# Recurrent mixer: two low halves on GpSimd, transfers reordered, last places filled by halves

## The chip, the cores and the metric

The kernel runs on one core of a Trainium2 chip. The metric is the device time of one execution in microseconds. The engines are TensorE (PE, with its weight loads as PEld), VectorE (DVE), ScalarE (ACT), GpSimd (POOL) and SyncE (SP), which issues all transfers.

## The reference

The reference is a stack of layers over x of 1 x 256 x 1024 in float32. First block: a mixer "ab", a routed feed-forward (moe0), a recurrent mixer (lru), a second routed feed-forward (moe1). Second block: twice a dense feed-forward, a pooling and attention mixer, and another dense feed-forward. The part around the change is:

```
# recurrent mixer: h = rms_norm(x)
gate, xr = split(h @ w_in); gate = gelu(gate)
xr = causal_conv(xr, conv_w) + conv_b              # 4 taps
r = sigmoid(xr @ w_a per head + b_a); i = sigmoid(xr @ w_x per head + b_x)
log_a = 8 r log_sigmoid(lam); a = exp(log_a)
b = sqrt(-expm1(2 log_a)) * (i * xr)
h_t = a_t h_{t-1} + b_t                            # over 256 positions
x = x + (gate * h) @ w_out
# routed stage: h = rms_norm(x); one group of 4, top 2 of its 8 experts
x = x + sum over the chosen experts of gate_e * (silu(h @ Wg_e) * (h @ Wu_e)) @ Wd_e
```

Each routed stage has 32 experts with three matrices of 2 MB each.

## The kernel before

Everything lives in SBUF with the channels on the 128 partitions. Dense weights come in chunks of 1 MB (`dense_chunks`, keys such as `("lru", 10)`), through a ring of six places: chunk number n lies in place n % 6. A chunk that is used in split precision is rounded by ScalarE to a high half (`hi`, L1238) and gets its low half by subtraction on VectorE (`lo`, L1670). `hi` counts `rounded` up, `lo` counts `remainder` up, per half f of the chunk, and TensorE then makes three products for each tile (`tile_products`, L570). The halves of the chunks of ab and lru lie in two pairs of buffers in turn. The chunks lru 8 and 9 are used as loaded, without halves (`whole_by_rows`, L775).

The lru stage: chunks lru 0 to 3 make the recurrent branch's input, `c_w_a` and `c_w_x` its gates, lru 4 to 7 the gelu branch, lru 8 to 11 the output projection. lru 4 to 7 lie in places 2 to 5, lru 8 to 11 in places 0, 1, 2 and 3. TensorE goes through lru 4 to 7 with the gates' products between them, then lru 8 and 9 together (L785: products for k 0 to 3 need gy 0 and gy 1, k 4 and 5 need gy 2, k 6 and 7 need gy 3), then lru 10 and lru 11. `gated(g)` on VectorE (L1876) makes gy g from the gelu branch (ScalarE, L1398) and the scan (L1913). All engines run in program order. VectorE's order at the end of the stage is scan 0, scan 1, gated 0, scaled_gate 3, gated 1, scan 2, gated 2, lo of lru 10 and 11, scan 3, gated 3, and then the low halves of gy. ScalarE's is four roots, four gelus, hi of lru 10 and 11, and the high halves of gy.

The routed stages read their 96 matrices each in a fixed order through about 13 places of 2 MB: expert rings, `work`, `spare_place`, and pairs of places of the dense ring (`EXTRA`, L464). `PLACES` (L470) lists which place each matrix takes. SyncE issues all of it in one order (`sp_program`, L2434): each issue waits until the last reader of its place is done. For the second routed stage it issues lru 4 to 7 with matrices 0 to 3 between them; then lru 8, 9, 10, 11 (`dense_load`, L2447; lru 8 and 9 wait for the gates' products, L2456); then matrix 4 when the low halves of lru 6 and 7 are made, 5 when those of lru 10 and 11 are made, 6 (in `work`) when all of gy and lru 9 are used, 7 when lru 8 and 9 are used, 8 and 9 after the products of lru 10 and 11 (`OUT_CHUNKS`, L465). The issues at L2490 are quarters of matrices that go out as TensorE frees parts of matrix 0. TensorE's products of the experts are L860 (gate, up) and L869 (down).

GpSimd does two sums at each routed stage (`first_sums`, L2419) and small work in the attention mixers.

Of the kernel before, what the change touches and what calls it, by code (L numbers as in the profile page):

```python
# [5 lines left out]
F32 = mybir.dt.float32  # L6
# [170 lines left out]
def build(nc, a, out, known):  # L177
# [14 lines left out]
    vec = signal("vec")  # L192
# [177 lines left out]
    for key in halved:  # L370
        held_before[key] = held_by.get(halves_of[key])
        held_by[halves_of[key]] = key
    splits = set(halved)

# [75 lines left out]
    def pair(ap, q):  # L452
        return ap[:, 2 * q:2 * q + 2, :]
# [79 lines left out]
    def pe_program(_):  # L533
# [36 lines left out]
        def tile_products(key, b, ready, x=h_halves, ks=range(KD), between=None):  # L570
            w = weights(key)
            for f in range(2):
                if f and between:
                    between()
                PE.wait_ge(remainder, key, f)
                for n, k in enumerate(ks):
                    PE.wait_ge(*ready(k))
                    ins = triple(bank[b][:, f * T:(f + 1) * T], [v[:, f, k, :] for v in w],
                                 [v[:, k, :] for v in x], n == 0, n == KD - 1)
                ins.then_inc(products.up(key, f), 1)  # L580
# [648 lines left out]
    def act_program(_):  # L1229
# [112 lines left out]
        def lru():  # L1342
            whole("lru")
            hi(("lru", 1))
            for q in range(4):
                gained("lru", q)
            table(ACTF.Sqrt)
            squares("lru")
            hi(("lru", 2))
            rms_later("lru", 3)  # L1350
            hi(("lru", 3))

            def first_tap(j):
                ACT.wait_ge(vec, "xr_in", j)
                for c in (2 * j, 2 * j + 1):
                    ins = S.activation(lru_xr[:, c, :], lru_pad[:, c, 0:T], ACTF.Identity, bias=small_of("c_conv_b", c, 1),
                                       scale=small_of("c_conv_w", c, 1))
                ins.then_inc(acted.up("tap", j), 1)

            def gates(g):  # L1360
                for m in range(2):
                    ACT.wait_ge(products, "gate", g, m)
                    ACT.wait_ge(vec, "half_b")
                    for f in range(2):
                        h = 2 * g + f
                        ins = S.activation((lru_ra, lru_bx)[m][:, h, :], bank[GATE_BANK[g % 2][m]][:, f * T:(f + 1) * T],
                                           ACTF.Tanh, bias=lru_cst[:, 4 + m, h:h + 1], scale=0.5)
                    ins.then_inc(acted.up("tanh", g, m), 1)
                ACT.wait_ge(acted, "tanh", g, 0)
                for h in (2 * g, 2 * g + 1):  # L1370
                    less = lru_cst[:, 1, h:h + 1]
                    ins = S.activation(hT[:, h, :], lru_ra[:, h, :], ACTF.Tanh, bias=less, scale=less)
                ins.then_inc(acted.up("less", g), 1)
                ACT.wait_ge(acted, "less", g)
                for h in (2 * g, 2 * g + 1):
                    c = lru_cst[:, 0, h:h + 1]
                    ins = S.activation(lru_ra[:, h, :], lru_ra[:, h, :], ACTF.Exp, bias=c, scale=c)
                ins.then_inc(acted.up("ra", g), 1)

            first_tap(0)  # L1380
            hi(("lru", 4))
            first_tap(1)
            table(ACTF.Tanh)
            hi(("lru", 5))
            gates(0)
            first_tap(2)
            first_tap(3)
            gates(1)
            hi(("lru", 6))
            gates(2)  # L1390
            hi(("lru", 7))
            gates(3)
            for g in range(4):
                ACT.wait_ge(vec, "factor", g)
                S.activation(pair(hT, g), pair(hT, g), ACTF.Sqrt).then_inc(acted.up("root", g), 1)
            for j in range(4):
                ACT.wait_ge(vec, "scaled_gate", j)
                S.activation(pair(lru_gate, j), pair(lru_gate, j), ACTF.Gelu_apprx_tanh).then_inc(acted.up("gelu", j), 1)  # L1398
            hi(("lru", 10))
            hi(("lru", 11))  # L1400
            for g in range(4):
                ACT.wait_ge(vec, "gy", g)
                ACT.wait_ge(products, ("lru", 7), 1)
                S.copy(pair(h_halves[0], g), pair(lru_gate, g)).then_inc(rounded.up("gy", g), 1)
            project("lru", 8, [])
# [263 lines left out]
    def dve_program(_):  # L1669
        def lo(key, halves=(0, 1)):  # L1670
            for f in halves:
                DVE.wait_ge(rounded, key, f)
                V.tensor_tensor(half_of(key, f, 1), tile_of(slot(key), key, f), half_of(key, f, 0).bitcast(F32),  # L1673
                                ALU.subtract).then_inc(remainder.up(key, f), 1)
# [158 lines left out]
        def lru():  # L1833
# [86 lines left out]
            gated(1)  # L1920
            scan(2)
            gated(2)
            lo(("lru", 10))
            lo(("lru", 11))
            scan(3)
            gated(3)
            for g in range(4):
# [470 lines left out]
    def pool_program(_):  # L2398
        def pools(s):

            POOL.wait_ge(vec, "ss", s)
            if s == "m1":
                POOL.wait_ge(vec, "merged", "m0", 3)
            for buf in (uT, s2, s4):
                ins = G.memset(buf[:, :, 0:EDGE], 0.0)
            pool_seq(ins, "edges", s)
            POOL.wait_ge(vec, "u", s, 4)
            src, dst = uT, s2
            for n, w in enumerate(WINDOWS):
                sh = w // 2  # L2410
                pool_seq(G.tensor_tensor(dst[:, n:, EDGE:L], src[:, n:, EDGE:L], src[:, n:, EDGE - sh:L - sh], ALU.add))
                G.tensor_scalar(poolT[:, n, EDGE:], dst[:, n, 2 * EDGE:L], 1.0 / w, None, ALU.mult)
                pool_seq(G.tensor_tensor(poolT[:, n, 0:EDGE], dst[:, n, EDGE:2 * EDGE],
                                         C("rcount")[:, n * EDGE:(n + 1) * EDGE], ALU.mult))
                pool_seq(G.tensor_tensor(poolT[:, n, :], poolT[:, n, :], uT[:, n, EDGE:L], ALU.subtract),
                         *(("pool", s) if n == 3 else ()))
                src, dst = dst, (s4 if dst is s2 else s2)

        def first_sums(s):  # L2419

            q = [work[:, EXP_F + i * 2 * T:EXP_F + (i + 1) * 2 * T] for i in range(3)]
            POOL.wait_ge(acted, "sq", s, 1)
            pool_seq(G.tensor_tensor(square_sum, q[0], q[1], ALU.add))
            POOL.wait_ge(acted, "sq", s, 2)
            pool_seq(G.tensor_tensor(square_sum, square_sum, q[2], ALU.add), "ss", s)

        for s in ROUTED:
            first_sums(s)
        for s in LATER:
            if s[0] == "m":  # L2430
                pools(s)


    def sp_program(_):  # L2434
# [128 lines left out]
        done = RING  # L2563
        for l in range(2):
            last = order.index(("ab", 13) if l == 0 else ("lru", 11)) + 1
            for i, n in enumerate(range(done, last)):
                dense_load(n)
                if i < 4:

                    if l:  # L2570
                        SP.wait_ge(products, *last_of(0, *PLACES[1][0][i]))
                    experts(l, i, i + 1)
            done = last
            n = 4
            for i, both in enumerate(EXTRA[l]):
                for d in both:
                    old = [k for k in order[:last] if place_of[k] == d][-1]
                    SP.wait_ge(products if old in AS_LOADED else remainder, old, 1)
                experts(l, n, n + 1)
                n += 1  # L2580
                if i == l:

                    if l == 0:
                        SP.wait_ge(remainder, "y", 3)
                    else:
                        SP.wait_ge(remainder, "gy", 3)
                        SP.wait_ge(products, ("lru", 9), 1)
                    experts(l, n, n + 1)
                    n += 1
            for i, key in enumerate(OUT_CHUNKS[l]):  # L2590
                SP.wait_ge(products, key, 1)
                experts(l, n, n + 1)
                n += 1
            second_half_of_first(l)
            last_quad = N_MATRIX - 2 * RING
            experts(l, n, last_quad)
            SP.wait_ge(vec, "flag", l)
            again(l, sync.value_load(most_tokens[0:1, l:l + 1], min_val=0, max_val=T))
            experts(l, last_quad, N_MATRIX)
            next_chunks(l, done, done + RING)  # L2600
            done += RING
# [71 lines left out]
```

## Time and profile before

| | us |
|---|---|
| median of 3 runs | 2076.36 |
| lowest and highest run | 2074.45, 2080.01 |
| the profiled execution | 2074.32 |
| its span | 2072.4 |
| PE, DVE, ACT, POOL busy | 1843.8, 1014.7, 703.5, 39.2 |
| mean transfer rate | 302 GB/s |

The profile is of one execution, its times counted from the start of the span. The lru stage lies from about 540 to 621 us, the second routed stage from there to about 1064 us. A busy share of TensorE near 1 does not say that TensorE is at its peak.

### The profile page before, as it was taken

The numbers are of one execution on the slowest core, as the hardware profiler recorded it, in microseconds if no ns is written. First come the engines' busy times: TensorE is split into PE (matmuls) and PEld (weight loads), VectorE is DVE, ScalarE is ACT, GpSimd is POOL, SyncE is SP. The second block draws the span as 40 slices with busy tenths as digits, with TensorE's granted clock in tenths as the row PEclk, the third lists the DMA queues.
The fourth block names the chain that finished last, engine by engine and source line by source line (L and its number), as shares of the span: only waits on it lengthen the run. The fifth ranks groups of instructions, "written<-read, shape, count | busy, mean of one in ns | idle before, by whom it ended". The sixth has DMA issues, their size and how long they took to land.

```text
span 2072.4 us, 31532 instructions
## 1 busy us (share of the span) xinstructions
PE 1843.8 (89%) x13948; PEld 1438.9 (69%) x13948; DVE 1014.7 (49%) x1434; ACT 703.5 (34%) x1049; POOL 39.2 (2%) x46
## 2 busy tenths in 40 slices
PE   9987776676998866677799999999999999999999
PEld 7944433344894433343478889998888888999888
DVE  5722110111672111011158777877777667787666
ACT  6310000000651000000055555655546445465553
POOL 0000000000000000000000003000000000300000
PEclk9999999989999999899899999999999999999999
DMA  9899999999979999999985554545555556445552
GB/s 397 338 415 429 430 430 431 430 429 425 407 323 419 430 430 429 430 431 430 426 326 194 192 207 174 182 170 185 184 204 193 190 183 216 175 160 183 186 195 88
DMA packets 64654, 626.59 MB, mean 302 GB/s; under 512 B 7168, under 2 KB 7296, under 8 KB 14464
## 3 DMA queue, kind: packets, MB, share of 16 engines
q1 hardware_dynamic: 64512, 624.50, 75.6%
q8 instruction: 113, 1.85, 0.3%
q14 instruction: 29, 0.24, 0.0%
HBM read 623.42 MB, written 1.05 MB: 301 GB/s over the span
## 4 chain that ended last, share of the span: by engine, by line
PE 72%; DMA 19%; DVE 4%; ACT 2%; SPq 2%; issue 1%; DVEq 0%; ACTq 0%
PE ps L606 14%; PE ps L609 7%; DMA dense_ring<-in_moe_w_down 7%; PE ps L869 7%; PE ps L550 6%; PE ps L552 6%; PE ps L551 6%; DMA expert_ring_a<-in_moe_w_down 5%; PE ps L860 5%; PE ps L1093 4%; PE ps L1072 4%; DMA work<-in_moe_w_down 3%; PE ps L849 3%; PE ps L885 3%; PE ps L1077 2%; PE ps L1097 2%
## 5 line engine op out<-in xcount | busy, mean ns | idle before, releaser
L1673 DVE TENSOR_TENSOR w_lo<-dense_ring,w_hi 128x1024 fp32r<-128x1024 f32 x398 | 468.9, 1222 | 54.8 <-ACT w_hi L1246 53.7
L1246 ACT CAST w_hi<-dense_ring 128x1024 fp32r<-128x1024 f32 x398 | 397.0, 1048 | 47.2 <-PE ps L552 26.1
L606 PE MATMUL ps<-h_both,w_hi 128*128 128x512 f32 x1344 | 337.3, 393 | 0.8 <-DVE work L2152 0.8
L606 PEld LDWEIGHTS ps<-h_both,w_hi 128*128 128x128 f32 x1344 | 241.8, 189 | 45.5 <-DVE work L2152 2.2
L2019 DVE TENSOR_TENSOR work<-work,ps 128x256 f32<-128x256 f32 x32 | 13.5, 421 | 484.4 <-ACT work L1437 484.4
L609 PEld LDWEIGHTS ps<-h_both,w_lo 128*128 128x128 f32 x1344 | 183.3, 190 | 13.1
L550 PE MATMUL ps<-h_both,w_hi 128*128 128x256 f32 x656 | 188.5, 287 | 0.4 <-DVE h_both L1679 0.3
L609 PE MATMUL ps<-h_both,w_lo 128*128 128x256 f32 x1344 | 187.4, 282 | 0.0
L552 PE MATMUL ps<-h_both,w_lo 128*128 128x256 f32 x656 | 185.6, 283 | 0.0
L551 PE MATMUL ps<-h_both,w_hi 128*128 128x256 f32 x656 | 185.6, 283 | 0.0
L1437 ACT ACTIVATE work<-ps 128x256 f32<-128x256 f32 x32 | 12.3, 384 | 484.6 <-PE ps L860 484.6
L860 PE MATMUL ps<-expert_ring_a,work 128*32 128x256 f32 x1216 | 114.6, 449 | 53.7 <-DMA expert_ring_a<-in_moe_w_up 29.2
L869 PE MATMUL ps<-dense_ring,work 128*32 128x512 f32 (+1 forms) x400 | 124.7, 559 | 16.3 <-DMA expert_ring_b<-in_moe_w_down 7.7
L550 PEld LDWEIGHTS ps<-h_both,w_hi 128*128 128x128 f32 x656 | 125.8, 192 | 1.9 <-DVE h_both L1679 0.8
L551 PEld LDWEIGHTS ps<-h_both,w_hi 128*128 128x128 f32 x656 | 125.8, 192 | 0.2
L552 PEld LDWEIGHTS ps<-h_both,w_lo 128*128 128x128 f32 x656 | 125.7, 192 | 0.0
L860 PEld LDWEIGHTS ps<-expert_ring_a,work 128*32 128x32 f32 x1216 | 61.2, 129 | 92.8 <-issue 74.2
L2152 DVE TENSOR_TENSOR work<-ps,work 128x512 f32<-128x512 f32 x87 | 60.1, 690 | 106.7 <-ACT work L1509 106.3
L860 PE MATMUL ps<-expert_ring_b,work 128*32 128x256 f32 x1088 | 88.1, 397 | 19.9 <-DMA expert_ring_b<-in_moe_w_gate 6.3
L869 PE MATMUL ps<-expert_ring_b,work 128*32 128x512 f32 (+1 forms) x288 | 92.1, 575 | 15.2 <-DMA expert_ring_b<-in_moe_w_down 9.3
L1509 ACT COPY work<-ps 128x512 f32<-128x512 f32 x87 | 50.9, 585 | 154.5 <-PE ps L609 154.1
L860 PE MATMUL ps<-dense_ring,work 128*32 128x256 f32 x992 | 99.3, 392 | 3.7 <-ACT work L1452 3.7
(319 smaller groups left out, 2852.1 us busy)
## 6 DMA issues: line engine op xcount, KB each, us to landing
dense_ring<-in_dense SPq DMA_DIRECT2D x207, 1024.0 KB, 4.9
expert_ring_b<-in_moe_w_up SPq DMA_DIRECT2D x20, 2048.0 KB, 39.9
expert_ring_a<-in_moe_w_gate SPq DMA_DIRECT2D x19, 2048.0 KB, 42.7
expert_ring_a<-in_moe_w_up SPq DMA_DIRECT2D x19, 2048.0 KB, 41.4
dense_ring<-in_moe_w_down SPq DMA_DIRECT2D x17, 2048.0 KB, 35.7
dense_ring<-in_moe_w_gate SPq DMA_DIRECT2D x17, 2048.0 KB, 39.9
expert_ring_b<-in_moe_w_down SPq DMA_DIRECT2D x14, 2048.0 KB, 44.8
dense_ring<-in_moe_w_up SPq DMA_DIRECT2D x14, 2048.0 KB, 40.0
```

The costliest lines, as they stand in the source:

```text
L550: mm(o, w[0], x[0], start=start, stop=False, **kw)
L551: mm(o, w[0], x[1], start=False, stop=False, **kw)
L552: return mm(o, w[1], x[0], start=False, stop=stop, **kw)
L606: mm(bank[b + f], w[0][:, f, k, :], h_pairs[:, k, :], start=k == 0, stop=False)
L609: ins = mm(bank[b + f][:, 0:T], w[1][:, f, k, :], h_halves[0][:, k, :], start=False, stop=k == KD - 1)
L849: ins = mm(bank[b][:, (k % 4) * P:(k % 4 + 1) * P], h_tok[:, tt * D + k * P:tt * D + (k + 1) * P], pick[:, tt * P:(tt + 1) * P], start=tt ...
L860: ins = mm(bank[2 + pr][c:c + CAP, m * half:(m + 1) * half], xs[:, k, (2 * pr + x) * CAP:(2 * pr + x + 1) * CAP], w[:, k, hf * half:(hf + ...
L869: return mm(bank[b][r0:r0 + CAP, cols], hidT[pr][:, c:c + CAP], w[:, parts, f, :], start=f == 0, stop=f == FE - 1)
L1072: mm(bank[4 + dt], w[0][:, f, dt * P:(dt + 1) * P], hid_pairs[:, 4 * j + f, :], start=j == f == 0, stop=False, skip_group_check=True)
L1093: mm(bank[E_BANK[s][c][f]], w[0][:, f, k, :], hid_pairs[:, r * KD + k, :], start=r == k == 0, stop=False, skip_group_check=True)
L1246: S.copy(half_of(key, f, 0), tile_of(slot(key), key, f)).then_inc(rounded.up(key, f), 1)
L1673: V.tensor_tensor(half_of(key, f, 1), tile_of(slot(key), key, f), half_of(key, f, 0).bitcast(F32), ALU.subtract).then_inc(remainder.up(key ...
```

## The change

Three things. The low halves of lru 10 and 11 are made by GpSimd instead of VectorE, and ScalarE rounds lru 10 ahead of its four gelus. SyncE issues lru 10 and 11 ahead of lru 8 and 9. And in the second routed stage matrix 5 is issued as two halves, the first when the low halves of lru 10 are made and the second when those of lru 11 are; the second half of matrix 6 goes out between them, after the last scan, and its first half where all of matrix 6 went. For the first routed stage the order is written anew but the same.

```diff
+    LESS_BY_POOL = [("lru", 10), ("lru", 11)]
 def tile_products(...)
-                PE.wait_ge(remainder, key, f)
+                PE.wait_ge(pooled if key in LESS_BY_POOL else remainder, key, f)
 ScalarE, lru()
+            hi(("lru", 10))
             for j in range(4):
                 ACT.wait_ge(vec, "scaled_gate", j)
                 S.activation(pair(lru_gate, j), pair(lru_gate, j), ACTF.Gelu_apprx_tanh)...
-            hi(("lru", 10))
             hi(("lru", 11))
 VectorE, lru()
             gated(2)
-            lo(("lru", 10))
-            lo(("lru", 11))
             scan(3)
 GpSimd
+        def less_of(key):
+            for f in range(2):
+                POOL.wait_ge(rounded, key, f)
+                G.tensor_tensor(half_of(key, f, 1), tile_of(slot(key), key, f), half_of(key, f, 0).bitcast(F32),
+                                ALU.subtract).then_inc(pooled.up(key, f), 1)
         for s in ROUTED:
+            if s == "moe1":
+                for key in LESS_BY_POOL:
+                    less_of(key)
             first_sums(s)
 SyncE
-            for i, n in enumerate(range(done, last)):
+            for i, n in enumerate(range(done, last) if l == 0 else [*range(done, last - 4), last - 2, last - 1, last - 4, last - 3]):
                 dense_load(n)
...
+            def emptied(d):
+                old = [k for k in order[:last] if place_of[k] == d][-1]
+                SP.wait_ge(products if old in AS_LOADED else pooled if old in LESS_BY_POOL else remainder, old, 1)
+            def by_halves(n, both, between=None):
+                for h, d in enumerate(both):
+                    emptied(d)
+                    piece(l, n, h, 2)
+                    if between and h == 0:
+                        between()
+            def late_work(n):
+                SP.wait_ge(vec, "scan", 7)
+                piece(l, n, 1, 2, last=0)
+            (first, second, third), w = EXTRA[l], n + 1 + l
...
+            else:
+                emptied(first[0])
+                emptied(first[1])
+                experts(l, n, n + 1)
+                by_halves(n + 1, second, lambda: late_work(w))
+                SP.wait_ge(remainder, "gy", 3)
+                SP.wait_ge(products, ("lru", 9), 1)
+                piece(l, w, 0, 2, last=0)
+            emptied(third[0])
+            emptied(third[1])
+            experts(l, n + 3, n + 4)
+            n += 4
```

## Rows read from the trace of the kernel before

**Rows 1.** The page, part 2: transfer rate in 40 equal slices of the span.
```profile
GB/s 397 338 415 429 430 430 431 430 429 425 407 323 419 430 430 429 430 431 430 426 326 194 192 207 174 182 170 185 184 204 193 190 183 216 175 160 183 186 195 88
```

**Rows 2.** Stretches: length, busy us of PE, PEld, DVE, ACT, POOL, clock, DMA share, GB/s.
```profile
574.50:579.50 5.00, 5.00 (x38) 4.79 (x37) 4.83 (x8) 4.97 (x10) 0.00 (x0) 1.00 0.08 20
...
594.50:599.50 5.00, 5.00 (x25) 4.40 (x24) 4.96 (x6) 2.12 (x4) 0.00 (x0) 1.00 0.04 16
...
605.00:607.00 2.00, 2.00 (x19) 2.00 (x18) 1.30 (x3) 0.63 (x1) 0.51 (x1) 1.00 0.73 156
607.00:633.00 26.00, 23.73 (x213) 20.88 (x213) 10.60 (x45) 7.00 (x15) 2.07 (x2) 1.00 1.00 425
633.00:636.00 3.00, 3.00 (x46) 2.15 (x50) 0.00 (x0) 1.93 (x3) 0.00 (x0) 1.00 0.83 270
...
700.00:1040.00 340.00, 244.30 (x2216) 130.47 (x2216) 40.42 (x84) 13.88 (x30) 0.00 (x0) 0.89 1.01 429
```

**Rows 3.** The chain of waits in the second routed stage: start, us, what.
```profile
897.71 36.49 DMA dense_ring<-in_moe_w_down
```

**Rows 4.** SyncE's longest wait (us, times, longest), then its issues: start, us, what.
```profile
SPq L2461 <- PE ps L753: 23.6, 1, 23.6
...
578.42 2.03 SPq L2461 DMA_DIRECT2D dense_ring<-in_dense  x4
...
605.03 0.33 SPq L2470 DMA_DIRECT2D work<-in_moe_w_gate  x1
...
610.73 7.87 SPq L2470 DMA_DIRECT2D expert_ring_b<-in_moe_w_up  x2
...
618.27 0.33 SPq L2470 DMA_DIRECT2D expert_ring_b<-in_moe_w_up  x1
...
630.89 0.33 SPq L2490 DMA_DIRECT2D expert_ring_a<-in_moe_w_down  x1
```

**Rows 5.** ScalarE, 583 to 596 us, in order of time: start, us, what.
```profile
586.61 1.28 ACT L1398 ACT_TABLE_LOAD   x1
587.90 1.67 ACT L1398 ACTIVATE work<-work 128x512 f32<-128x512 f32 x3
...
591.20 3.87 ACT L1246 CAST w_hi<-dense_ring 128x1024 fp32r<-128x1024 f32 x4
```

**Rows 6.** VectorE, 588 to 602 us, in order of time.
```profile
588.87 0.67 DVE L1876 TENSOR_TENSOR work<-work 128x512 f32<-128x512 f32 x1
...
593.85 4.63 DVE L1673 TENSOR_TENSOR w_lo<-dense_ring,w_hi 128x1024 fp32r<-128x1024 f32 x4
...
600.49 0.69 DVE L1876 TENSOR_TENSOR work<-work 128x512 f32<-128x512 f32 x1
```

**Rows 7.** TensorE, products of lru 8 and 9, then the first of lru 10.
```profile
589.73 10.55 PE L785 MATMUL ps<-work,dense_ring 128*128 128x256 f32 x48
601.23 3.72 PE L785 MATMUL ps<-work,dense_ring 128*128 128x256 f32 x16 [0.95 <-DVE work L1876]
604.60 0.47 PE L550 MATMUL ps<-h_both,w_hi 128*128 128x256 f32 x1
```

**Rows 8.** First attention mixer: GpSimd and VectorE in order of time; GpSimd's sums by line.
```profile
1275.02 1.89 POOL L2411 TENSOR_TENSOR scratch<-scratch 128x1024 f32<-128x1024 f32 x1 [23.76 <-DVE scratch L2340]
...
1275.10 3.17 DVE L2265 TENSOR_TENSOR scratch<-scratch,work 128x1280 f32<-128x1280 f32 x1
...
L2423 POOL TENSOR_TENSOR work<-work 128x512 f32<-128x512 f32 x2 | 2.6, 1291 | 600.3 <-ACT work L1252 600.3
```

**Rows 9.** Transfers issued at 598.5, 618.3 and 630.9 us: KB, us from issue to landing.
```profile
dense_ring<-in_moe_w_down SPq DMA_DIRECT2D x1, 2048.0 KB, 8.0
...
expert_ring_b<-in_moe_w_up SPq DMA_DIRECT2D x1, 2048.0 KB, 9.9
...
expert_ring_a<-in_moe_w_down SPq DMA_DIRECT2D x1, 512.0 KB, 6.4
```

More of the change, by code:

```diff
@@ L2574, in sp_program @@
             n = 4
[L2575 to L2578, printed above, removed]
-                experts(l, n, n + 1)
[L2580 to L2589, printed above, removed]
+            def emptied(d):
[11 more added lines that the diff above has]
+            (first, second, third), w = EXTRA[l], n + 1 + l
+            if l == 0:
+                emptied(first[0])
+                emptied(first[1])
+                experts(l, n, n + 1)
+                SP.wait_ge(remainder, "y", 3)
+                experts(l, w, w + 1)
+                emptied(second[0])
+                emptied(second[1])
+                experts(l, n + 2, n + 3)
+            else:
+                emptied(first[0])
+                emptied(first[1])
+                experts(l, n, n + 1)
[7 more added lines that the diff above has]
+            n += 4
             for i, key in enumerate(OUT_CHUNKS[l]):
```

## The prediction

> **What bounds the kernel now.** I read the rate of the transfers over the span first. In the first half the core loads at about 430 GB/s in most slices, in the second half at about half that [rows 1]. The change lies in the recurrent mixer (540 to 621 us), ahead of the second routed stage. That stage is bound by loading: from 700 to 1040 us the DMA engines are busy without a gap at 429 GB/s while TensorE works 244.30 of 340 us [rows 2], and the chain of waits goes through transfers of 36 us each, once per quad of experts [rows 3]. So its end is the end of one stream of transfers. A microsecond in which that stream stands still is lost, unless the stream is held up again later for a reason that the change does not touch: then only the last hold-up counts.
>
> The stretches [rows 2] show where it stands still: 5.0 us at 20 GB/s, 5.0 us at 16 GB/s and 2.0 us at 156 GB/s. Against 429 GB/s that is 4.8 + 4.8 + 1.3 = 10.9 us. From 607 to 633 us it runs at 425 GB/s, and from 633 to 636 us at 270 GB/s once more (3.0 x (1 - 270/429) = 1.1 us).
>
> SyncE's queue tells why [rows 4]. It stood 23.6 us in one wait, for the gates' products, and issued nothing until 578.42 us; then it waited for low halves of chunks (matrix 5 goes out at 598.5 us) and for output products (605.03, 610.73, 618.27 us). The issue at 630.89 us waits for TensorE's first expert products.
>
> **The change, part by part.** (1) Chunks lru 10 and 11 are issued ahead of lru 8 and 9. Their places were emptied by the low halves of lru 4 and 5, which VectorE makes before `factors(0)`, long before 578 us. Two chunks are 2.1 MB, 4.9 us at 429 GB/s: they run in the first hole. lru 8 and 9 come next and start no later than now, since their own wait sets them. Gain in the stream at this point 4.8 us.
>
> (2) ScalarE rounds lru 10 before the gelus. The roots end at 586.6 us, a table load of 1.28 us follows, and the gelus start at 587.90 us [rows 5]. Two roundings of 0.97 us each (3.87 for four) go in front: table load 588.6 to 589.9, first gelu done at about 590.5. VectorE's `gated(0)`, now started at 588.87 us [rows 6], waits for it. Without more, gy 0 is there at 591.2 instead of 589.5 us, and TensorE, which starts the output products at 589.73 us with no gap [rows 7], starts 1.5 us later. Queued behind this wait on VectorE are `scaled_gate(3)`, `gated(1)` and the scans.
>
> (3) VectorE loses four subtractions, 4.63 us [rows 6]. `gated(3)`, now at 600.49 us, moves forward by it. TensorE waits for it only 0.95 us, between its 48 and its last 16 matmuls [rows 7]: this is all that TensorE can gain from part 3. With parts 2 and 3 alone it reaches lru 10 at 604.60 + 1.5 - 0.95 = 605.1 us, 0.5 us late.
>
> (4) GpSimd makes the four halves. No row has this shape on it; the nearest two: 128x1024 in 1.89 us, and 128x512 in 1.29 us, twice that is 2.6 us [rows 8]. I take 1.9, the row of the same size, and keep 2.6 as the other end. Their own end (about 600 us) is early enough for TensorE, which needs them after 604 us. What matters is what they do to VectorE. VectorE's 128x1280 instruction started 0.08 us after GpSimd's 1.89 us one and took 3.17 us [rows 8]; at the 1.16 us per 1024 of the four subtractions [rows 6] it takes 1.5 alone. It stood still for 1.7 us: the two engines did not read together, and VectorE waited out the whole GpSimd instruction. Nearly all of VectorE's instructions here (scan, `gated`) have both inputs in SBUF, as that one had; `scaled_gate`, from PSUM, has one.
>
> [...]
>
> So, in turn: the first high half is rounded at 587.6; GpSimd gets in when the running scan ends, 588.3, and holds until 590.0; VectorE's last scan of the pair runs to 590.6; GpSimd's second holds until 592.3; `gated(0)` ends at 592.95. TensorE starts at 593.0 instead of 589.73: 3.3 us. It needs gy 2 after 7.0 us (600.0) and gy 3 after 10.55 us (603.5). VectorE and GpSimd take turns again for lru 11 (rounded at 595.2 and 596.1, since the fourth gelu goes first): gy 2 at about 600.0, gy 3 at 602.9, in time. TensorE is late by 3.3 - 0.95 = 2.3 us. With the 2.6 us price `gated(0)` ends 1.4 us later, gy 2 comes at about 603.0 against 601.4 needed and gy 3 at about the end of those products, less the turns: 5.3 us late. Without the exclusion 0.5.
>
> (5) Places filled by halves. First half of matrix 5 at about 592.4, second half of matrix 6 after the last scan (602), second half of 5 at about 602, first half of 6 with the wait for lru 9. Each issue costs SyncE 0.33 us, and it is otherwise waiting. These 3 MB fill part of the second and third hole.
>
> What is late next decides. Matrix 8 and 9 and the pieces at 630.89 us are issued when TensorE is done, so these move with it. How much was in the queue then? An issue into an empty queue takes 8.0 us to land (2 MB, 598.5 us); the one at 618.27 us took 9.9: it found 1.9 us of work ahead. The 512 KB at 630.89 us took 6.4 [rows 9]; an empty queue would be 8.0 less 1.5 MB at 429 GB/s (3.7), 4.3 to 4.9: at most 2.1, 1.5 likely. But the rate fell to 270 GB/s just there, which says the queue was running dry: 0 is the other end. I take 0.8. A fuller stream ahead of 618 us can therefore not be carried past 631 us by more than that reserve. Whatever the holes give beyond is lost again, as an empty queue that waits for TensorE.
>
> **Sum.** Stream end after = +(TensorE's delay) - (reserve) = 2.3 - 0.8 = +1.5 us. Ends: 0.5 - 1.5 = -1.0 and 5.3 - 0 = +5.3. Later stages are unchanged and follow. The profiled execution took 2074.32 us (span 2072.4, 1.9 outside): 2075.8. The median shown is 2.0 us higher, 2076.36, within the 5.6 us between its runs; I forecast for it 2077.9 us. About 0.3% (6.2 us) is what a measurement can tell from no change: this is no change.
>
> **Rivals.** A: the hole counts in full. All 10.9 us come out (2065.5), or the 4.8 of part 1 (2071.6). For it: the stage is bound by the stream. Against it: the reserve at 618.27 and 630.89 us, which only an earlier TensorE can raise, and TensorE can gain 0.95 at most. 4 in 100.
> B: slower. The exclusion is dearer: GpSimd's instructions hold 2.6 us or get in before each of VectorE's, so that gy 0, gy 2 and gy 3 are each late. The price is 5.3 us on the forecast's side of the reserve, 2081.7; it counts from a delay of TensorE above the reserve, and passes 0.3% above 7 us. For it: the 1.29 us row. 14 in 100.
> C: no exclusion for scans, or GpSimd in the gaps of VectorE: delay 0.5, -1.0 to +0.5, 2075.4 to 2076.9. Against it the 3.17 us row. 16 in 100.
> D: the change does not do what it says: lru 10 lands or is rounded no earlier in effect (its half place in ScalarE's order still waits for lru 6's products), and all stays within 0.5 us of 2076.4. Against it: those products end near 584 us. 4 in 100.
>
> **How the numbers follow.** Forecast 62 in 100; its own range 2076 to 2080. The range 2073.4 to 2082 takes in C, D and B's price, and the runs' own spread; A and the worst of B are outside. Faster by over 0.3%: A's upper half and stray runs, 0.03. Slower: B beyond 7 us and stray runs, 0.07. Same: 0.90.
>
> **What would show it.** Step 1: no hole at 574 to 579 us. Step 2: first gelu about 2 us later. Step 4: scans or `gated` of VectorE that take 2 us and more beside GpSimd; four GpSimd rows of about 2 us. TensorE's first output product near 593 us and no gap of 0.95 us before the last 16. The holes at 594 and 605 us smaller, a new one near 620 or a longer one near 634 us. From 700 us on the same picture shifted by 1 to 2 us. I am wrong if the second routed stage ends over 2 us earlier, or if TensorE is more than 5 us late at lru 10.

## The result, and the profile after

The changed kernel takes 2080.43 us (median of 13 runs, 2079.47 to 2082.57), the one before 2075.36 us over 13 runs beside it (2073.14 to 2080.01). The ratio, formed from the runs beside each other, is 1.0026, 95% interval 1.0018 to 1.0033: 5.4 us slower. That is just under the 0.3% (6.2 us) named in the prediction, and with this many runs clear of zero. The time lies in the range of 2073.4 to 2082 us, but 0.4 us above the forecast's own 2076 to 2080; the forecast 2077.9 us had 1.5 of the 5.4 us.

The span went from 2072.4 to 2077.9 us. The first view is the one of stretches, of the kernel after; its columns are those of [rows 2].

```profile
574.50:579.50 5.00, 5.00 (x38) 4.79 (x37) 4.83 (x8) 4.97 (x10) 0.00 (x0) 1.00 0.97 377
594.50:599.50 5.00, 5.00 (x13) 3.98 (x12) 4.86 (x5) 3.09 (x5) 3.82 (x2) 0.50 0.36 149
599.50:605.00 5.50, 5.50 (x27) 4.83 (x27) 5.36 (x7) 1.54 (x3) 1.27 (x1) 1.00 0.17 31
607.00:633.00 26.00, 25.65 (x189) 23.87 (x188) 9.96 (x35) 5.22 (x10) 2.58 (x2) 0.93 0.93 371
...
637.00:639.00 2.00, 2.00 (x25) 1.30 (x24) 0.91 (x5) 0.37 (x1) 0.00 (x0) 1.00 0.70 256
700.00:1040.00 340.00, 248.92 (x2236) 133.12 (x2232) 40.40 (x84) 13.85 (x30) 0.00 (x0) 0.88 1.01 429
```

The first hole is filled: 377 GB/s where it was 20. The stream stands still later instead, 31 GB/s from 599.5 to 605 us, where it ran at 372 before, and from 607 to 633 us it moves 371 GB/s against 425. From 700 us on it is busy at 429 GB/s, as before. New is TensorE's clock: 0.50 from 594.5 to 599.5 us, where it was 1.00 before. The 0.93 in the stretch from 607 to 633 us is a second, shorter fall, from 626.9 to 630.1 us.

The next fences are VectorE, GpSimd and ScalarE of the kernel after, in order of time (start, us, what); they answer to [rows 6], [rows 8] and [rows 5].

```profile
587.21 5.61 DVE L1914 TENSOR_TENSOR_SCAN work<-work 128x256 f32<-128x256 f32 x2
592.74 0.66 DVE L1877 TENSOR_TENSOR work<-work 128x512 f32<-128x512 f32 x1
593.33 0.68 DVE L1881 TENSOR_TENSOR work<-ps,rinv 128x512 f32<-128x512 f32 x1
...
595.24 3.39 DVE L1914 TENSOR_TENSOR_SCAN work<-work 128x256 f32<-128x256 f32 x2
598.73 2.59 DVE L1877 TENSOR_TENSOR work<-work 128x512 f32<-128x512 f32 x1
...
603.33 0.69 DVE L1877 TENSOR_TENSOR work<-work 128x512 f32<-128x512 f32 x1
```

```profile
587.18 2.39 POOL L2430 TENSOR_TENSOR w_lo<-dense_ring,w_hi 128x1024 fp32r<-128x1024 f32 x1 [494.30 <-ACT w_hi L1247]
589.54 2.73 POOL L2430 TENSOR_TENSOR w_lo<-dense_ring,w_hi 128x1024 fp32r<-128x1024 f32 x1
595.68 2.40 POOL L2430 TENSOR_TENSOR w_lo<-dense_ring,w_hi 128x1024 fp32r<-128x1024 f32 x1 [3.41 <-ACT w_hi L1247]
```

```profile
586.01 1.98 ACT L1247 CAST w_hi<-dense_ring 128x1024 fp32r<-128x1024 f32 x2
588.01 1.28 ACT L1400 ACT_TABLE_LOAD   x1
589.30 1.67 ACT L1400 ACTIVATE work<-work 128x512 f32<-128x512 f32 x3
```

Two scans that take 0.69 and 0.67 us when VectorE is alone took 5.61 us beside two GpSimd subtractions of 2.39 and 2.73 us, and the first of them started 0.03 us after GpSimd. The first gelu was done at 589.9 us: `gated(0)`, at 592.74 us, waited for the scans and not for it.

TensorE, of the kernel after:

```profile
593.55 16.97 PE L786 MATMUL ps<-work,dense_ring 128*128 128x256 f32 x64 [4.14 <-DVE work L1877]
610.16 0.47 PE L551 MATMUL ps<-h_both,w_hi 128*128 128x256 f32 x1
```

TensorE stood 4.14 us, then needed 16.6 us from its first output product to lru 10, against 10.55 + 3.37 = 13.9 us of work before [rows 7]. The 0.95 us wait ahead of the last 16 is gone. So lru 10 begins 5.9 us later: 4.14 - 0.95 + 2.7 (20.75 us after the end of lru 7, against 14.87). With no wait at all and the clock kept, the same products take 13.7 us (e6, below), so the lost gap is worth 1.2 us and the fallen clock 2.9; the sum is the same. The last row of the routed stage in the chain of waits (start, us), of the kernel before and after:

```profile
1056.86 6.91 PE ps L799 x32
```

```profile
1062.33 6.91 PE ps L800 x32
```

From lru 10 to this end it is 459.2 us before and 459.1 after. As far as one profile of each can tell, the whole loss stands between lru 7 and lru 10, and none of it was absorbed. How full the queue of transfers was tells why; those issued at 616.3, 623.8 and 636.8 us after (KB, us to landing), the last two answering to [rows 9]:

```profile
expert_ring_b<-in_moe_w_up SPq DMA_DIRECT2D x1, 2048.0 KB, 11.0
...
expert_ring_b<-in_moe_w_up SPq DMA_DIRECT2D x1, 2048.0 KB, 8.5
...
expert_ring_a<-in_moe_w_down SPq DMA_DIRECT2D x1, 512.0 KB, 5.1
```

8.5 us where an empty queue takes 8.0, and 5.1 where 4.3 to 4.9 was worked out: both found the queue all but empty.

A little more goes with the second fall of the clock. From lru 10 to the first issue that waits for TensorE's first expert products (L2490 before, L2499 after) it is 26.29 us before and 26.67 after, 0.4 us longer.

### The profile page after: what moved, and what is told of

It reads as the page before. It is cut to its first block, busy times and chain, and to the rows that moved or that the text cites. A ratio compares the mean times of both kernels' runs of the same rounds, so it can differ in the third digit from the quotient of the medians.

```text
span 2077.9 us, 31529 instructions
## 1 busy us (share of the span) xinstructions
PE 1852.6 (89%) x13944; PEld 1444.2 (70%) x13948; DVE 1018.5 (49%) x1430; ACT 703.4 (34%) x1049; POOL 49.4 (2%) x50
## 4 chain that ended last, share of the span: by engine, by line
PE 72%; DMA 19%; DVE 5%; ACT 2%; SPq 2%; issue 1%; DVEq 0%; ACTq 0%
PE ps L607 14%; PE ps L610 7%; PE ps L870 7%; DMA dense_ring<-in_moe_w_down 7%; PE ps L551 5%; PE ps L553 5%; PE ps L552 5%; DMA expert_ring_a<-in_moe_w_down 5%; PE ps L861 5%; PE ps L1094 4%; PE ps L1073 4%; DMA work<-in_moe_w_down 3%; PE ps L850 3%; PE ps L886 3%; PE ps L1078 2%; PE ps L1098 2%
```

## The experiments

The table gives for each kernel two times of its profile. "To lru 10" runs from the end of lru 7's products to the first product of lru 10 on TensorE, as the difference to the 14.87 us of before. "Stage" runs from there to the end of the second routed stage, as the difference to 459.2 us. Each comes from one profile. Stage lengths of kernels that I would call alike differ by up to about 1 us, so I read nothing into less. Where TensorE waited right behind lru 7 (the change, e2, e4, e5, e7), counting from the start of lru 7's last product instead of its end would add 0.16 us to the first column. The last column is the ratio of times to the kernel before with its 95% interval. The edits below are shortened; that of e6 shows VectorE's order against the kernel before.

| kernel | to lru 10 | stage | ratio |
|---|---|---|---|
| the change | +5.9 | -0.1 | 1.0026 (1.0018 to 1.0033) |
| e1: gelus first | +5.4 | -0.7 | 1.0019 (1.0010 to 1.0029) |
| e2: lows on VectorE | +1.0 | +1.2 | 1.0004 (0.9994 to 1.0014) |
| e3: transfers alone | 0.0 | -1.0 | 1.0004 (0.9995 to 1.0013) |
| e4: TensorE kept busy | +3.9 | -0.8 | 1.0020 (1.0010 to 1.0030) |
| e5: GpSimd only writes | +0.2 | -0.9 | 0.9997 (0.9988 to 1.0007) |
| e6: last scan first, changed transfers | -1.2 | -0.1 | 0.9992 (0.9983 to 1.0001) |
| e7: GpSimd in quarters | +0.2 | -0.9 | 1.0001 (0.9992 to 1.0010) |
| e8: before, TensorE late | +4.6 | +0.8 | 1.0025 (1.0015 to 1.0034) |
| e9: last scan first alone | -1.2 | +3.9 | 1.0010 (1.0001 to 1.0019) |
| e10: quarters, gelus first | -1.2 | +3.5 | 1.0009 (1.0000 to 1.0018) |
| e11: e6 again | -1.2 | -0.5 | 0.9990 (0.9981 to 0.9999) |
| e12: e6 with halves only | -1.2 | -0.2 | 0.9996 (0.9987 to 1.0005) |

**e1, gelus first.**
```diff
-            hi(("lru", 10))                       # ahead of the four gelus
+            hi(("lru", 10)); hi(("lru", 11))      # behind them, as before
```


> The changed kernel, with ScalarE's rounding of lru 10 behind the gelus again. Theory (GpSimd's subtractions keep VectorE's instructions with two SBUF inputs waiting, 2.2 us each): the loss stays and only moves. gy 0 and gy 1 are there by 591.2 us as before and TensorE starts its output products without a gap; but the four subtractions now fall on scans 4 to 7 and on gy 2 and gy 3, so TensorE waits about 4 us for gy 2 in the middle of them, and the kernel is 4 to 6 us slower than the one before. Rival (the order on ScalarE is what costs, since gated(0) waits for the first gelu): with the gelus first the loss is gone, within 1 us of the kernel before.

The loss stayed and moved. VectorE and TensorE of e1:

```profile
593.77 3.42 DVE L1914 TENSOR_TENSOR_SCAN work<-work 128x256 f32<-128x256 f32 x2
597.30 2.59 DVE L1877 TENSOR_TENSOR work<-work 128x512 f32<-128x512 f32 x1
599.81 2.84 DVE L1912 TENSOR_TENSOR work<-work,hT 128x512 f32<-128x512 f32 x1
602.69 3.30 DVE L1914 TENSOR_TENSOR_SCAN work<-work 128x256 f32<-128x256 f32 x2
```

```profile
591.64 7.10 PE L786 MATMUL ps<-work,dense_ring 128*128 128x256 f32 x32
599.95 3.72 PE L786 MATMUL ps<-work,dense_ring 128*128 128x256 f32 x16 [1.20 <-DVE work L1877]
606.83 5.41 PE L786 MATMUL ps<-work,dense_ring 128*128 128x256 f32 x16 [3.17 <-DVE work L1877]
```

TensorE starts without a gap and waits for gy 2 (1.20 us) and gy 3 (3.17 us) instead. I had put about 4 us on gy 2 alone; the waits together come to 4.4 us. Behind the second one the clock fell, which I had not expected:

```profile
608.00:611.50 3.50, 3.50 (x10) 2.77 (x9) 2.50 (x5) 1.57 (x3) 0.00 (x0) 0.52 0.96 396
```

The last 16 products took 5.41 us instead of 3.72, and this 1.7 us is part of the 5.4. The order on ScalarE is not the cause.

**e2, low halves on VectorE.**
```diff
-    LESS_BY_POOL = [("lru", 10), ("lru", 11)]
+    LESS_BY_POOL = []
             gated(2)
+            lo(("lru", 10)); lo(("lru", 11))
             scan(3)
```


> The changed kernel, with the four low halves on VectorE again, where they stood before (after gated(2)); the early rounding of lru 10, the order of the transfers and the halves stay. Theory of the exclusion: no scan over 0.7 us; the first gelu ends near 590 us, gy 0 near 590.7, TensorE starts 1.0 to 1.5 us late, its clock does not fall, and it is 0.0 to 0.6 us late at lru 10; the time is within 1.5 us of the kernel before. Rival (the transfers cost: halves and the new order leave the queue empty at the wrong moment): still 3 us or more slower than before.

As the theory had it: scans of 1.27 us for two, TensorE waits 1.39 us for gy 0 and 0.46 us ahead of the last 16, and its clock stays at 1.00 through these products. It is 1.0 us late at lru 10, more than the 0.0 to 0.6 expected. Taking GpSimd out takes nearly the whole loss away. This is also the price of the early rounding by itself, with the low halves on VectorE: 1.0 us on TensorE. Later, in the routed stage, the clock did fall for 6.6 us, where before it is 1.00:

```profile
622.00:628.50 6.50, 6.28 (x32) 5.33 (x33) 4.42 (x21) 1.74 (x4) 0.00 (x0) 0.50 0.97 388
```

From lru 10 to the first issue that waits for expert products it is 27.29 us here against 26.29: 1.0 of the 1.2 us by which this stage is longer. e6 (27.48 us) and e11 (27.43) have the same long fall, e1 one like the change's (26.69). In all the others it is 26.3 us, also in e3, e9 and e12, whose clock fell there for about 3 us.

**e4, TensorE kept busy in its wait.**
```diff
                     if j == 0:
                         claim(2, vec, "x", s, 1)
+                        keep_awake(18, 0)     # 18 products of zeros ahead of the output products
```


> The changed kernel, with 18 products of zeros on TensorE (about 3.9 us) in its wait for gy 0, so that it does not idle. Theory: of the 5.5 us that TensorE is late at lru 10, the exclusion gives 3.5 and the lower clock after the idle 4.1 us gives 2. [...] Rival (the clock does not matter, since gy 2 and gy 3 set the end of these products): no gain, 5 us slower than before.

TensorE of e4:

```profile
590.89 3.83 PE L548 MATMUL ps<-zeros 128*128 128x512 bf16 x17
594.97 7.14 PE L787 MATMUL ps<-work,dense_ring 128*128 128x256 f32 x32 [0.25 <-DVE work L1878]
602.80 7.17 PE L787 MATMUL ps<-work,dense_ring 128*128 128x256 f32 x32 [0.69 <-DVE work L1878]
```

The clock is 1.00 from 589 to 610 us, the products take 7.14 + 7.17 us and the wait for gy 2 is 0.69 us. I had expected 0.7 us of wait, about 14.8 us for the products with the wait in it, TensorE 3.5 to 4 us late and a kernel about 2 us faster than the changed one. (17 of the 18 products of zeros are in the trace.) lru 10 begins 3.9 us late instead of 5.9. So the fallen clock costs 2.0 us net, and the rest of the change 3.9, of which 0.2 stay without the exclusion (e5). In the times the step from 1.0026 to 1.0020 is 1.2 us where 2 was expected, inside both intervals; the split rests on the traces.

**e5, GpSimd writes only.**
```diff
-                G.tensor_tensor(half_of(key, f, 1), tile_of(slot(key), key, f), half_of(key, f, 0).bitcast(F32),
-                                ALU.subtract).then_inc(pooled.up(key, f), 1)
+                G.memset(half_of(key, f, 1).bitcast(F32), 0.0).then_inc(pooled.up(key, f), 1)
```


> The changed kernel, where GpSimd writes zeros into the four low halves instead of subtracting (the low halves of lru 10 and 11 are left out of the result). GpSimd then reads nothing from SBUF. Theory (the two engines exclude each other in reading): scans of 0.7 us, TensorE starts about 1 us late and loses no clock, within 1.5 us of the kernel before, maybe 1 us faster since no low half is on VectorE. Rival (any GpSimd instruction on SBUF keeps VectorE waiting for its length): scans lengthened by the length of a GpSimd write. Rival (order on ScalarE or transfers cost): still 4 us slower.

VectorE, GpSimd and TensorE of e5:

```profile
589.04 1.27 DVE L1914 TENSOR_TENSOR_SCAN work<-work 128x256 f32<-128x256 f32 x2
```

```profile
588.99 1.84 POOL L2430 MEMSET w_lo<- 128x1024 f32 x2 [496.07 <-ACT w_hi L1247]
```

```profile
592.63 14.05 PE L786 MATMUL ps<-work,dense_ring 128*128 128x256 f32 x64 [1.39 <-DVE work L1877]
```

The writes run from 588.99 us right beside the two scans, and these take 1.27 us as alone. So neither GpSimd's being at work nor its writing, 0.95 us for each half, held VectorE up here. Its subtractions differ from the writes in that they read SBUF, compute, and take longer. Length is not it, since a subtraction of 0.74 us in e7 (next) held up a scan too; whether it is the reading or the computing, no run shows. The loss is gone with everything else of the change in place: order on ScalarE, transfers, halves.

**e7, GpSimd in quarters.**
```diff
+                for k in range(0, KD, 2):     # four subtractions of 128x256 in place of one of 128x1024
+                    ins = G.tensor_tensor(half_of(key, f, 1)[:, k:k + 2, :], tile_of(slot(key), key, f)[:, k:k + 2, :],
+                                          half_of(key, f, 0)[:, k:k + 2, :].bitcast(F32), ALU.subtract)
+                ins.then_inc(pooled.up(key, f), 1)
```


> The changed kernel with each of GpSimd's four subtractions cut into four instructions of 128x256. Theory (VectorE waits for the GpSimd instruction that runs, not for all of them): each scan or product of VectorE waits 0.4 to 0.8 us instead of 2.2, gy 0 comes 2 us earlier than in the changed kernel, TensorE idles about 2 us and keeps its clock, is 1.5 to 2.5 us late at lru 10, and the kernel is 3 us faster than the changed one. [...]

VectorE and GpSimd of e7:

```profile
587.94 2.35 DVE L1914 TENSOR_TENSOR_SCAN work<-work 128x256 f32<-128x256 f32 x2
```

```profile
587.92 17.49 POOL L2431 TENSOR_TENSOR w_lo<-dense_ring,w_hi 128x256 fp32r<-128x256 f32 x16 [495.15 <-ACT w_hi L1247]
```

The two scans wait 0.5 us each instead of 2.2. gy 0 then waits for its gelu (0.42 us more), TensorE idles 1.39 us, its clock stays, and it is 0.2 us late, less than the 1.5 to 2.5 expected. By the ratios, 5.2 us of the change's 5.4 come back (1.0001), where I had expected 3. VectorE waited for the GpSimd instruction that ran, and for no more: the first scan took 1.27 us beside a quarter of 0.74 us, the second 1.16 us beside one of 1.12 us. The four subtractions take GpSimd 17.49 us in this form, against 5.1 us for each two (10.2 in all) in the changed kernel.

**e8, the kernel before with TensorE late.**
```diff
+                        keep_awake(27, 0)     # nothing of the change
```


> The kernel before, nothing of the change, with 27 products of zeros (5.8 us) on TensorE ahead of its first output product. TensorE is then 5.8 - 0.95 = 4.9 us late at lru 10, with its clock kept. Theory (the end of the stage moves with TensorE, less a small reserve of the queue of 0.4 to 0.8 us): 4 to 4.5 us slower than before, as the changed kernel is for its delay. Rival (the changed kernel's loss is in its transfers): this one loses less than 2 us, since its queue is fed as before.

27 products of zeros took 6.00 us and lru 10 began 4.6 us late. The ratio is 1.0025, 5.2 us (3.1 to 7.1): about as much as the change cost, with the old transfers. A delay of TensorE here is paid in full as far as this can tell; its interval does not part a reserve of 0 from the 0.8 us that I took.

**e3, the changed transfers alone.**
```diff
-    LESS_BY_POOL = [("lru", 10), ("lru", 11)]     # lows on VectorE, gelus first, as before
+    LESS_BY_POOL = []
```


> The kernel before with the changed transfers alone: lru 10 and 11 issued ahead of lru 8 and 9, matrix 5 and 6 as halves; rounding and low halves as before. Theory (the stream is tied to TensorE again at 618 and 631 us, so a fuller stream ahead of that is lost again): the hole at 574 to 579 us is gone, 4.8 us of transfers more are done by 590 us, and the time is the same within 1 us. Rival (a filled hole counts in full): 4 to 5 us faster.

The first hole was at 398 GB/s instead of 20, and the time did not move (1.0004). The filled hole brings nothing that these runs can tell.

**e6 and e11, the last scan first.**
```diff
             gated(2)
-            lo(("lru", 10)); lo(("lru", 11))
             scan(3); gated(3)
+            lo(("lru", 10))
             for g in range(4):
                 lo_pair(("gy", g), h_halves, lru_gate, g)
+            lo(("lru", 11))
```


> Changed transfers, gelus first, the low halves on VectorE, but in another order: scan 3 and gated(3) at once after gated(2), then the low halves of lru 10, those of gy, and those of lru 11 last. No GpSimd. Theory (TensorE's time at lru 10 sets the stage): gy 3 is there by 597 us, the 0.95 us gap ahead of the last 16 output products is gone, TensorE reaches lru 10 1 us earlier than before, and the kernel is 0.5 to 1.0 us faster than before. Rival (matrix 5 now goes out 2 to 5 us later and the queue runs dry): same or 1 us slower.

**e9, this order alone, with the transfers as before.**

> The kernel before with VectorE's new order alone (scan 3 and gated(3) ahead of the low halves of lru 10, those of lru 11 last); the transfers as before. TensorE loses its 0.95 us gap, as in the version with both. Theory (TensorE's time sets the stage, the filled hole brings nothing): as fast as the version with both, 0.5 to 1.5 us faster than before. Rival (the moved transfers are what keeps the queue fed when matrix 5 goes out later, here at 603.5 us): 2 to 4 us slower than the version with both, since matrix 5 is then issued 5 us later than before and all of it lies behind.

> Both parts: the changed transfers and VectorE's order with the last scan first, no GpSimd, on the same chip as the order alone. Theory: 0.5 to 1.7 us faster than before, no difference from the order alone beyond 0.5 us. Rival (the transfers matter once TensorE is earlier): 2 us or more faster than the order alone.

In all three TensorE goes through its output products without a wait and is 1.2 us early. With the changed transfers that is 0.9992 and 0.9990, on two chips; the second interval lies below 1. It has the lowest ratio of the study: by the medians 1.5 to 1.7 us faster than the kernel before, and by the ratios about 7 us faster than the change. Alone the order is slower than before, and 3.6 us slower than e11 beside it (medians 2077.67 and 2074.05): my theory that the transfers do not matter fell here. The low halves of lru 11 now come after those of gy, so matrix 5, which waits for them, goes out at 603.9 instead of 598.5 us, with 6, 7 and all others behind it. The transfer issued at 617.4 us in e9 and the one at 618.9 us in e11:

```profile
expert_ring_b<-in_moe_w_up SPq DMA_DIRECT2D x1, 2048.0 KB, 14.7
```

```profile
expert_ring_b<-in_moe_w_up SPq DMA_DIRECT2D x1, 2048.0 KB, 10.2
```

In e9 it finds 6.7 us of work ahead, in e11 2.2. The queue is no longer held up by TensorE in e9 but by its own late start, and the stage is 3.9 us longer.

**e12, halves without the reordering.**
```diff
-            for i, n in enumerate(range(done, last) if l == 0 else [*range(done, last - 4), last - 2, last - 1, last - 4, last - 3]):
+            for i, n in enumerate(range(done, last)):     # otherwise e6
```


> VectorE's order with the last scan first and the transfers by halves, but lru 10 and 11 issued behind lru 8 and 9 as before: the hole at 574 to 579 us is open again, and the 4.8 us of transfers come after it. Theory (the halves, issued near 601 us ahead of TensorE's end at 604 us, are what keeps the queue from being the last hold-up; the order of the four chunks only fills a hole whose gain is lost again): as fast as the version with both, 0.5 to 2 us faster than before. Rival (the order of the chunks is what matters): like VectorE's order alone, 2 us slower than before.

The stretch 574.5 to 579.5 us of e12 is a hole again:

```profile
574.50:579.50 5.00, 5.00 (x38) 4.79 (x37) 4.83 (x8) 4.97 (x11) 0.00 (x0) 1.00 0.09 39
```

And yet its stage is as long as e6's and e11's, and its time within their intervals, 0.9996 against 1.0010 for the order alone. What e9 lacked were the halves, 2 MB that go out near 600 us, ahead of TensorE's end. The order of the four chunks adds nothing that these runs can tell.

**e10, quarters with the gelus first.**

> The changed kernel with GpSimd's subtractions in quarters and the gelus ahead of the rounding of lru 10. TensorE starts its output products without a gap. GpSimd works from about 592 us, so scans 4 to 7 and gy 2 and gy 3 wait 0.3 to 0.6 us per instruction: gy 2 near 596.5 (needed near 596.7), gy 3 near 601 (needed near 600.3). Theory: TensorE within 1 us of the kernel before at lru 10, the time the same within 1 us, no better than the order on VectorE alone. Rival (quarters free GpSimd's help of its price): 1.5 us or more faster than before.

TensorE was 1.2 us early, more than expected, and the kernel still no faster than before (1.0009, interval 1.0000 to 1.0018; beside e11 its median is 3.4 us longer). GpSimd in quarters was done with lru 11 only at 608.8 us: SyncE issued the second half of matrix 5 at 608.92 us, with matrix 7 behind it. As in e9 the stream's own start became the last hold-up (+3.5 us), a thing that the expectation had not looked at.

## Why the prediction was right or wrong

The verdict of no change by 0.3% and the range held; the size was 3.9 us short: the sum gave a loss of 1.5 where 5.4 was measured. The direction and the path (GpSimd's subtractions, VectorE, TensorE, stream) were right. That the verdict held is in part luck: 5.4 us is 0.8 short of the 6.2 that the prediction drew as its line, much less than the error. By the prediction's own sign it was wrong, since TensorE is 5.9 us late at lru 10 and it named more than 5 as that sign. By its steps:

Part 1: lru 10 and 11 filled the first hole as said, and brought nothing (e3, e12). Right, and the runs fit the reason given, that the last hold-up counts.

Part 2: the first gelu was done at 589.9 us, 590.5 forecast, but it set nothing; the scans did. With part 3 and without the exclusion, forecast at 0.5 us, it cost 0.2 (e5). With the low halves on VectorE it costs 1.0 us (e2).

Part 3: taken 0.95 us on TensorE, 1.2 measured with no gap left (e6). A term of the right kind and nearly the right size.

Part 4: that VectorE waits for GpSimd's subtractions was right and is shown (e2 and e7; e5 shows that writes alone did not hold it up). That this holds for the scan, and that GpSimd waits for a scan that runs (588.3 us in the sum), was my assumption: no row of before shows either. In the changed kernel the scans took 2.92 and 2.77 us instead of 0.69 and 0.67; GpSimd's first subtraction started 0.03 us ahead of its scan and waited for none, and the second, started while a scan ran, took 2.73 us against 2.39. The term was too small. First, the price of one subtraction: taken 1.89 us from the row of the same width, measured 2.39. Twice the 1.29 us row (2.6) would have been nearer; why the row of the same width was not, no run shows. Two at 0.5 us more fit the step from the wait of 3.3 us forecast to the 4.14 measured. Second, the term that the sum did not have: when TensorE had stood 4.1 us its clock was granted at 0.50 for some 7 us, and the output products took 2.7 us longer, 2.0 of it net (e4), since at a clock of 1.00 they waited 0.69 us for gy 2. This term was put at nothing, without a word on it. The 0.95 us gap of before had cost no clock (1.00, the last 16 products in 3.72 us [rows 7]), and I did not ask what a longer one does.

Part 5: the halves cost nothing that can be told (e3, e5, e7). That they pay as soon as the low halves of lru 11 come later (e9 against e12) was not seen.

The reserve: taken 0.8 us, with 0 as the other end. The stage after lru 10 was 459.1 us in the changed kernel, against 459.2 before and 460.0 with TensorE late (e8). That says 0, and so does the drop to 270 GB/s at 633 us [rows 2], but it isn't shown to better than 1 us: the stages of e3, e4, e5 and e7, which have the changed transfers too, are 0.8 to 1.0 us shorter than before, and about 0.4 us of the changed kernel's stage goes with its second fall of the clock.

With 2.39 us, the clock and no reserve the sum is 4.1 - 0.95 + 2.7 - 0 = 5.9 on TensorE, and 5.5 in the span, since lru 7 ended 0.3 us earlier than before. Rival B, the dearer exclusion, came nearest with its 5.3 us, in part by luck: its price of 2.6 us was near the 2.39, but it had TensorE with no loss of clock waiting for gy 2 and gy 3, and the clock took that place. Rival C failed on the 5.61 us of two scans, A on e3, D on the filled hole and the early rounding.

What stays open: why e8's stage is 0.8 us longer than before, beside a noise of about 1 us; and why the clock fell near 621 us in e2, e6 and e11, though TensorE had been busy up to there.

## What to carry to other kernels

Work moved to GpSimd was not free for VectorE here: GpSimd's subtractions held up VectorE's instructions with two inputs in SBUF, each for about as long as the GpSimd instruction ran (a scan took 2.92 us instead of 0.69 beside one of 2.39 us); writes alone did not (e5, two scans in 1.27 us). If such work must go there, try it in short instructions (0.5 us of wait for each of two scans in e7, instead of 2.2), look at what it does to the instructions ahead of the critical engine, and check that GpSimd is still done in time: in quarters it was not (e10, done at 608.8 us). A hole in a stream of transfers was worth here what the last hold-up after it left: 398 GB/s instead of 20 for 5 us brought nothing (e3, 1.0004). Look at how much work each later issue finds in the queue, move that last hold-up first, and then check which one has become the last. A wait added to TensorE can have a second price in its clock: after waits of 4.14 and 3.17 us it was granted 0.50 here, after one of 1.39 us 1.00.

## What the runs showed of the hardware that was not expected

TensorE stood 4.14 us and was granted 0.50 of its clock from about 592.7 to 599.5 us: the fall came while it still stood, and lasted 6 us into its work. After 3.17 us (e1) it was granted 0.50 from 608.0 to about 611.8 us. Through the products behind idle gaps of 1.39 us (e2, e5, e7) and 0.95 us (before) it kept 1.00, and with zeros in the gap too (e4). A gap is not needed for a fall: in e2 TensorE was busy from 612 to 622 us, and the clock was 0.50 from there to 628.6 us.

In the changed kernel GpSimd's subtractions held up a tensor_tensor_scan (2.92 and 2.77 us instead of 0.69 and 0.67) like a tensor_tensor (2.59 us instead of 0.69, at 598.73 us). GpSimd waited too: its second subtraction took 2.73 us against 2.39 for the first, behind the scan that had got in between.

A product of VectorE with one input from PSUM was not held up in e7. It ran in the middle of a GpSimd subtraction and took 0.68 us as alone; VectorE and GpSimd:

```profile
591.32 0.68 DVE L1881 TENSOR_TENSOR work<-ps,rinv 128x512 f32<-128x512 f32 x1
```

```profile
590.78 1.21 POOL L2431 TENSOR_TENSOR w_lo<-dense_ring,w_hi 128x256 fp32r<-128x256 f32 x1
```

But one input was not enough to be free of it in e10. There four tensor_scalar instructions, with their one large input in SBUF, took about 0.8 us each beside GpSimd's 0.74 us subtractions, where the same line (L1723 before) takes 0.35. The first two of them:

```profile
605.29 1.56 DVE L1724 TENSOR_SCALAR hT<-xT,small 128x256 f32<-128x256 f32 x2
```
